# The first loads of a two-block transformer kernel reordered by fourths, with sixteen unread identity products

## The reference

```
mod      = silu(c) @ ada_w + ada_b          # 1024 -> 6144, for c and for c_ctx
h        = rms_norm(x, g) * (1 + scale) + shift     # shift, scale: columns of mod
q, k, v  = split(h @ w_qkv)                 # 1024 x 3072, for x and for ctx
```

## Time and profile before

| | us |
|---|---|
| profiled execution, whole | 1554.06 |
| its span, first to last instruction | 1552.5 |
| TensorE busy | 1519.2 (98%) |
| VectorE busy | 938.1 (60%) |
| ScalarE busy | 705.3 (45%) |
| mean granted clock of TensorE, share of full | 0.997 |

### The profile page before, as it was taken

One profiled execution on the slowest core, in us unless ns is written; L12 is line 12 of the kernel. 1 busy time (PEld: TensorE's weight loads), 2 busy tenths in 40 slices (PEclk: granted clock), 3 DMA queues, 4 the chain that ended last, 5 costly groups with the idle time before them and its releaser, 6 DMA issues.

```text
span 1552.5 us, 21801 instructions
## 1 busy us (share of the span) xinstructions
PE 1519.2 (98%) x9159; PEld 1265.9 (82%) x9159; DVE 938.1 (60%) x1238; ACT 705.3 (45%) x972; POOL 82.0 (5%) x116
## 2 busy tenths in 40 slices
PE   6999999999999999999999999999999999999998
PEld 4777656878888888879778888899988899988887
DVE  5422587463434343356866666678798856679973
ACT  4311475242312222235764545545556546556553
POOL 2010043000000000000010000034000000000000
PEclk8999999999999999999999999999999999999999
DMA  9665432654432332364144555665565554555652
GB/s 360 233 204 166 139 45 73 237 190 136 164 107 82 109 108 69 123 238 142 55 136 136 182 178 177 214 210 184 166 194 186 182 188 149 186 189 179 192 188 81
DMA packets 244161, 251.39 MB, mean 162 GB/s; under 512 B 17134, under 2 KB 237649, under 8 KB 244065
## 3 DMA queue, kind: packets, MB, share of 16 engines
q1 hardware_dynamic: 242528, 247.48, 49.0%
q0 software_dynamic: 928, 1.87, 0.4%
q10 hardware_dynamic: 608, 0.66, 0.1%
HBM read 248.94 MB, written 1.05 MB: 161 GB/s over the span
## 4 chain that ended last, share of the span: by engine, by line
PE 73%; DVE 14%; ACT 5%; issue 2%; POOL 2%; DMA 1%; SPq 1%; POOLq 0%; DVEq 0%; ACTq 0%
PE psum L367 71%; DVE wl L353 6%; ACT wh L346 3%; PE psum L948 2%; DVE scr L2105 1%; DVE scr L2102 1%; DVE scr L2116 1%; DVE scr L2114 1%; DMA pre<-in_ada_w 1%; DVE vsum L2112 1%; ACT scr L2046 1%; DVE sums L1004 1%; POOL ptmp L1868 1%; DMA bias<-in_na_rpb 1%; SPq L293 0%
## 5 line engine op out<-in xcount | busy, mean ns | idle before, releaser
L353 DVE TENSOR_TENSOR wl<-raw,wh 128x2048 fp32r<-128x2048 f32 (+1 forms) x185 | 417.9, 2261 | 261.0 <-ACT wh L346 260.7
L346 ACT ACTIVATE wh<-raw 128x2048 fp32r<-128x2048 f32 (+1 forms) x185 | 347.9, 1883 | 348.7 <-PE psum L367 338.0
L367 PE MATMUL psum<-x,wh 128*128 128x512 f32 (+1 forms) x1440 | 438.8, 365 | 0.8 <-DVE x L549 0.8
L367 PE MATMUL psum<-x,wl 128*128 128x256 f32 x1248 | 350.0, 280 | 0.0
L367 PEld LDWEIGHTS psum<-x,wh 128*128 128x128 f32 x1440 | 258.2, 189 | 46.3 <-issue 1.8
L367 PE MATMUL psum<-xh,wh 128*128 128x512 f32 (+1 forms) x688 | 259.8, 378 | 0.7 <-DVE xl L701 0.7
L367 PE MATMUL psum<-xl,wh 128*128 128x512 f32 (+1 forms) x688 | 255.5, 371 | 0.0
L367 PE MATMUL psum<-xh,wl 128*128 128x512 f32 (+1 forms) x688 | 255.2, 371 | 0.0
L367 PEld LDWEIGHTS psum<-x,wl 128*128 128x128 f32 x1248 | 236.6, 190 | 0.0
L367 PEld LDWEIGHTS psum<-xh,wh 128*128 128x128 f32 x688 | 130.2, 189 | 33.0 <-issue 5.0
L367 PEld LDWEIGHTS psum<-xh,wl 128*128 128x128 f32 x688 | 130.2, 189 | 22.3
(11 more groups left out here) (279 smaller groups left out, 2027.0 us busy)
## 6 DMA issues: line engine op xcount, KB each, us to landing
raw<-in_ffn_w_in SPq DMA_DIRECT2D x44, 1024.0 KB, 5.0
pre<-in_ada_w SPq DMA_DIRECT2D x25, 1024.0 KB, 10.5
raw<-in_ada_w SPq DMA_DIRECT2D x23, 1024.0 KB, 5.7
raw<-in_w_ffn_gate SPq DMA_DIRECT2D x22, 1024.0 KB, 5.1
raw<-in_w_ffn_up SPq DMA_DIRECT2D x22, 1024.0 KB, 5.1
raw<-in_w_ffn_down SPq DMA_DIRECT2D x19, 1024.0 KB, 5.0
raw<-in_ffn_w_out SPq DMA_DIRECT2D x16, 1024.0 KB, 5.0
raw<-in_na_w_qkv SPq DMA_DIRECT2D x12, 1024.0 KB, 5.2
```

The source lines that it names most:

```text
L346: act.e.activation(wh[:, c % NSPL, 0:z], raw[:, p % NRAW, 0:z], ACT.Copy).then_inc(W.hi, 1)
L353: dve.e.tensor_tensor(wl[:, c % NSPL, 0:z], raw[:, p % NRAW, 0:z], wh[:, c % NSPL, 0:z].bitcast(F32), ALU.subtract).then_inc(W.lo, 1)
L367: return pe.e.matmul(o, l, r, start=start, stop=stop, skip_group_check=shared)
```

## The change

The loads are issued in the order x, ctx, ada 0 and 1, a fourth of w0 and w1, ada 2 and 3, a fourth, ada 4 and 5, a fourth, ada 6, ada 7, the last fourth, then w2 and on. A fourth is two k-tiles of both chunks (two loads of 256 KB). The splits follow in fourths (`first_weights`), counted on `J0` for the first three and on `W.hi` and `W.lo` for the last. x is transposed when it has landed, ctx afterwards, in pairs of k-tiles that VectorE copies alone. In TensorE's queue chunks 2 and 3 of `ada_w` go behind the first two k-tiles of c = 0, and so on for each batch. Behind fold 0 stand sixteen products of the identity with itself that nobody reads. `J0` is also used in the second attention layer, where its counts now begin at 6 (`KH`).

```
+            def load_quarter(b):
+                if b >= 2:
+                    sp.wait_ge(J0.hi, 2 * b - 2)
+                for c in range(2):
+                    w, src = (t[:, 2 * b:2 * b + 2, :] for t in (view(raw, c, weights[c]), weights[c][0]))
+                    sp.e.dma_start(w, src).then_inc(s_raw[b % 2], 16)
             for p, (kind, x) in enumerate(dma):
-                if p == 1:
-                    load_staged((2, 3))
-                elif p == 2:
-                    load_staged((4, 5, 6))
+                if p < 2:
+                    continue
+                if p == 2:
+                    for b in range(3):
+                        load_staged((2 * b, 2 * b + 1))
+                        load_quarter(b)
+                    load_staged((6,))
+                elif p == 3:
+                    load_quarter(3)
...
         def setup_pe():
             pe.wait_ge(L.cst, 16)
-            pe.wait_ge(L.row0, 64)
-            pe.e.transpose(bank[6][:, 0:P], vrow[:, 0, :], ident).then_inc(C.turned, 1)
-            pe.wait_ge(L.x, 16)
-            pe.wait_ge(L.ctx, 16)
-            for f in range(KT):
...
+            for a, landed in enumerate((L.x, L.ctx)):
+                pe.wait_ge(landed, 16)
+                for q in range(4):
+                    if a:
+                        pe.wait_ge(X.hT, q + 1)
+                    for m in range(2):
+                        for t in range(2):
...
+                if a == 0:
+                    pe.wait_ge(L.row0, 64)
+                    pe.e.transpose(bank[6][:, 0:P], vrow[:, 0, :], ident).then_inc(C.turned, 1)
             spread_pe(0, 4)
             ada_mm(0)
             ada_mm(1)
             ada_fold(0)
-            ada_mm(2)
-            ada_mm(3)
+            for i in range(16):
+                mm(bank[6][:, 256:384], ident, ident, True, True)
...
         # ScalarE, for each batch b
-            split_hi(0)
+            def first_weights(c, b):
+                q = slice(512 * b, 512 * b + 512)
+                act.wait_ge(s_raw[b % 2], 32 * (b // 2 + 1))
+                act.e.activation(wh[:, c, q], raw[:, c, q], ACT.Copy).then_inc(J0.hi if b < 3 else W.hi, 1)
             for b in range(4):
-                if b == 3:
-                    split_hi(2)
                 modulation(b)
-                if b == 1:
-                    split_hi(1)
+                for c in range(2):
+                    first_weights(c, b)
                 for k in (2 * b, 2 * b + 1):
                     first_high(k)
+            split_hi(2)
...
         # VectorE
+            unmodulated(0)
+            unmodulated(1)
             for b in range(4):
-                if b == 3:
-                    split_lo(2)
                 ada_add(b)
                 first_coefs(b)
...
+                first_normed(2 * b)
+                first_weights(0, b)
+                first_low(2 * b)
+                first_normed(2 * b + 1)
+                first_low(2 * b + 1)
+                first_weights(1, b)
+                if b < 3:
+                    unmodulated(2 * b + 2)
+                    unmodulated(2 * b + 3)
+            split_lo(2)
...
         # qkv0_first_pe
+            for b in range(4):
+                part(0, 2 * b)
+                last = part(0, 2 * b + 1)
+                if b < 3:
+                    ada_mm(2 * b + 2)
+                    ada_mm(2 * b + 3)
+                    part(1, 2 * b)
+                    ada_fold(b + 1)
+                else:
+                    last.then_inc(W.used, 1)
+                    ada_pe(0)
+                    part(1, 2 * b)
+                last = part(1, 2 * b + 1)
+            last.then_inc(W.used, 1)
             ada_pe(1)
```

More of the change, by code:

```diff
@@ L278, in program, with landed @@
         W = semaphores(nc, "w", "hi lo used")
+        def landed(p):
+            return 16 * (p // NRAW + 1) + (48 if p % NRAW < 2 else 0)
         def view(t, slot, src):
@@ L575, in program @@
         C = semaphores(nc, "c", "turned vt act dve")
-        X = semaphores(nc, "x", "tile hT_d hT_a square hn")
+        J0 = semaphores(nc, "split", "hi lo")
+        X = semaphores(nc, "x", "tile hT square hn")
         cf = ins["conv_ffn_2"].rearrange("l k (m p) -> (l k m) p", p=P)
@@ L605, in setup_pe @@
             pe.wait_ge(L.cst, 16)
-            pe.wait_ge(L.row0, 64)
-            pe.e.transpose(bank[6][:, 0:P], vrow[:, 0, :], ident).then_inc(C.turned, 1)
-            pe.wait_ge(L.x, 16)
-            pe.wait_ge(L.ctx, 16)
-            for f in range(KT):
[L611 to L615, removed]
+            for a, landed in enumerate((L.x, L.ctx)):
[5 more added lines that the diff above has]
+                        for t in range(2):
+                            f = 2 * q + m
+                            last = pe.e.transpose(bank[q][:, m * T + t * P:m * T + t * P + P], vtok[:, 2 * a + t, f * P:(f + 1) * P], ident)
+                    last.then_inc(X.tile, 1)
+                if a == 0:
+                    pe.wait_ge(L.row0, 64)
+                    pe.e.transpose(bank[6][:, 0:P], vrow[:, 0, :], ident).then_inc(C.turned, 1)
             spread_pe(0, 4)
@@ L642, in setup_act @@
             act.e.activation(cz[:, :, 30:32].rearrange("p k s -> p s k"), sc.rearrange("p (s k) -> p s k", s=2), ACT.Copy).then_inc(C.act, 1)
-            for f in (5, 7):
-                act.wait_ge(X.tile, f + 1)
-                act.e.activation(hT[:, f, :], bank[f % 4][:, :], ACT.Copy).then_inc(X.hT_a, 1)
             def first_high(k):
@@ L673, in setup_dve @@
             dve.e.tensor_reduce(four[:, :], ident.rearrange("p (j r) -> p r j", j=4), AX.X, ALU.add).then_inc(C.dve, 1)
[L674 to L681, removed]
+            for a in range(2):
+                for q in range(4):
+                    dve.wait_ge(X.tile, 4 * a + q + 1)
+                    dve.e.tensor_copy(hT[:, 2 * q:2 * q + 2, a * T:a * T + T], two(bank[q])).then_inc(X.hT, 1)
+                    if a and q == 1:
+                        recip_dve(0, 4)
+                if a == 0:
+                    dve.wait_ge(C.turned, 1)
+                    dve.e.tensor_copy(vt[:, 0:P], bank[6][:, 0:P]).then_inc(C.vt, 1)
             dve.wait_ge(N.spread, 1)
-            dve.wait_ge(X.tile, KT)
             def unmodulated(k):
-                dve.wait_ge(X.hT_d, min(k + 1, 6))
-                dve.wait_ge(X.hT_a, (k >= 5) + (k >= 7))
+                dve.wait_ge(X.hT, 5 + k // 2)
                 dve.e.tensor_tensor(hn[:, k, :], hT[:, k, :], stat[:, :], ALU.mult).then_inc(X.hn, 1)
@@ L711, in first_normed, with first_weights @@
                                         ALU.add).then_inc(N.scaled, 1)
-            for k in range(4):
-                unmodulated(k)
-            split_lo(0)
+            def first_weights(c, b):
+                q = slice(512 * b, 512 * b + 512)
+                if b < 3:
+                    dve.wait_ge(J0.hi, 2 * b + c + 1)
+                else:
+                    dve.wait_ge(W.hi, c + 1)
+                dve.e.tensor_tensor(wl[:, c, q], raw[:, c, q], wh[:, c, q].bitcast(F32), ALU.subtract).then_inc(J0.lo if b < 3 else W.lo, 1)
+            unmodulated(0)
+            unmodulated(1)
             for b in range(4):
-                if b == 3:
-                    split_lo(2)
                 ada_add(b)
                 first_coefs(b)
[L721 to L731, removed]
+                first_normed(2 * b)
[8 more added lines that the diff above has]
+            split_lo(2)
         B = semaphores(nc, "bias", "in0 in1 masked hi lo")
@@ L765, in qkv0_first_pe, with part @@
             out_ = bank[0:2], bank[2:4]
[L767 to L773, removed]
-                return last
[L776 to L792, removed]
+            def part(c, k):
+                if k >= 6:
+                    h, l = taken(c)
+                else:
+                    pe.wait_ge(J0.lo, k // 2 * 2 + c + 1)
+                    h, l = (view(t, c, weights[c]) for t in (wh, wl))
+                pe.wait_ge(N.xl, 2 * k + 2)
+                for m in range(2):
+                    w = slice(m * P, (m + 1) * P)
+                    last = three(out_[c][m][:, :], h[:, k, w], l[:, k, w], xh0[:, k, :], xl0[:, k, :], k == 0, k == KT - 1)
+                return last
+            for b in range(4):
+                part(0, 2 * b)
+                last = part(0, 2 * b + 1)
+                if b < 3:
+                    ada_mm(2 * b + 2)
+                    ada_mm(2 * b + 3)
+                    part(1, 2 * b)
+                    ada_fold(b + 1)
+                else:
+                    last.then_inc(W.used, 1)
[3 more added lines that the diff above has]
+            last.then_inc(W.used, 1)
             ada_pe(1)
@@ L1047, in program @@
         A0 = semaphores(nc, "att", ATT)
-        J0 = semaphores(nc, "split", "hi lo")
         units0 = [(2 * p + (kind > 0), 2 if kind == 0 else 1, max(kind - 1, 0), 4 * p + (0, 2, 3)[kind]) for p in range(8) for kind in range(3)]
```

7 lines of the change are left out of this document (3 added, 4 removed).

## The result

Thirteen runs of each kernel in turn gave 1558.94 us (1556.78 to 1561.13) for the changed kernel and 1555.62 us (1553.09 to 1556.69) for the one before. The ratio is 1.0026, 95% interval 1.0019 to 1.0033: slower, by 4 us (the medians lie 3.3 us apart). The profiled execution took 1558.94 us with a span of 1557.1, 4.6 us over the span of before.

What follows compares the result with a forecast made beforehand. TensorE, 98% busy, bounds the kernel; only the first 60 us could change. Earlier start and full clock, less batch and load waits, put w2 at 62.2 instead of 58.9: +3.3 on 1555.1 gives 1558.4 us, range 1556.6 to 1560.6 (all cases 1554.0 to 1562.5).

Steps and rivals of the forecast that it cites:

- sixteen products: On TensorE behind fold 0: 1.8 us at the high clock, 16.5 to 18.3, ahead of the first w0 product, costing nothing.
- first w0 product (S0): Start of the first batch's first product on TensorE: at 19.3 us instead of 25.9.
- one batch: Cycle from one batch's first product to the next: 9.38 us, with TensorE waiting 1.3 us for VectorE.
- F3: Moment of VectorE's add behind fold 3, on which w2's late load depends: 44.9 us.
- wait for ada 8: TensorE idle for 4.1 us from 50.3, until ada 8 lands at about 54.4 behind w2.
- wait for ada 9: Second idle stretch of TensorE, 2.5 us from 58.4, until ada 9 lands at 60.9.
- w2's products: First matmul with weight chunk 2, the milestone after which nothing is touched: 62.2 instead of 58.9, +3.3 us.
- the late clock: Rival: low clock before the first w0 product or at ada 9, or a late first load; +6.3, 1561.4 us, chance 0.17.
- Its second form: Clock still low when ada 9 comes, at the first stage's end: up to 1.5 us, within a rival of chance 0.17.
- The chain inside a batch does not bind: Rival: VectorE's and ScalarE's steps overlap better, a cycle takes 8.1 us; +0.7, 1555.8 us, chance 0.12.
- Faster: Rival: late w2, ada 8 and ada 9 loads do not bind the first stage; -3.5, 1551.6 us, chance 0.11.
- The fourth: Rival: before's slower time comes from the first stage's clock, which the change avoids; +3.3 becomes +1, 1557.4 us, chance 0.12.

Runs made afterwards that it cites:

- one: The kernel before with only w2's load issued late and its split at the end of the first stage: 1560.25 us against 1552.80, ratio 1.0048.
- two: The changed kernel with ada 7, 8 and 9 loaded into the buffers of ada 0, 1 and 2, and w2 into raw 2: 1551.45 us, ratio 0.9989 to before.
- ten: The changed kernel with only the fold moved ahead of both k-tiles of c = 1: 1555.78 us against 1554.06 for before, ratio 1.0013.
- nine: The changed kernel with staged loads, eight products and the fold ahead of both k-tiles of c = 1: 1547.79 us, ratio 0.9960 to before.
- three to eight: The changed kernel with none, eight, sixteen, none, eight products, then eight with staged loads; ratios to before 1.0045, 1.0026, 1.0038, 1.0033, 1.0032, 0.9982.
- seven: The changed kernel with eight identity products instead of sixteen, timed again on a second chip: 1557.60 us against 1552.25 for before, ratio 1.0032.

## Why the prediction was right

| step | predicted | changed kernel |
|---|---|---|
| sixteen products | 1.8, hidden | 3.58 (16.68 to 20.26), 0.8 to 0.9 in sight |
| first w0 product (S0) | 19.3 | 20.26 |
| one batch | 9.38 | 9.47, 9.49, 9.48 |
| F3 | 44.9 | 46.08 |
| w2 issued | 46.8 | 48.05 |
| w2 from issue to use | 4.89 | 4.76 |
| its split until ada 9's issue | 4.3 | 4.31 |
| ada 9 from issue to use | 4.89 | 5.25 |
| wait for ada 8 | 4.1 | 4.24 |
| wait for ada 9 | 2.5, less what a low clock takes | 0.80, with 1.7 for the low clock |
| w2's products | 62.2 (+3.3) | 63.56 (+4.6) |

The mechanism held in every step of this profile, and the direction. The first product came early by what was forecast less the products, the batches waited for VectorE, and the time was set by a load, a split and a load behind fold 3. Experiments one, two and ten show the late loads, nine and ten the wait inside a batch, and three to eight what the products cost and keep.

Not all of the nearness is merit. The forecast time, 1558.4 us, is only 0.5 under the measured one, but the milestone moved by 4.6 us where 3.3 were forecast. The medians moved by 3.3 and the ratio says 4.0; with 3 us of noise behind the milestone that agreement is partly luck. The prediction itself gave "slower" a chance of 0.44, no more than "same".

The term that was mis-sized is the sixteen products, 1.8 us instead of 3.58. I priced a product of the identity as a transpose. The trace counts x32 for sixteen: a plain fp32 matmul is two there, each 0.11 us. The rows held this already. A fold is two products in the code and stands as x4, and a pair of `ada_mm` is sixteen in the code and stands as x32. With 3.6 us S0 would have been 20.1, the sum +4.1, and the forecast nearer. It also moved the cover: the products end behind the low part that they fill the time for, so the last 0.8 us of them are on the path. The other misses are the batches (+0.1 each), VectorE's steps behind F3 (1.97 instead of 1.87) and ada 9's load (+0.36), less the small -0.13 of w2's. Some working of the prediction was loose, without weight for the result: 60.9 + 1.0 + 0.2 is 62.1 and not 62.2, and the parts that it gives for its range of +1.5 to +5.5 add up to +2.0 to +6.3.

The clock fell behind the wait of 4.24 us, and in the changed kernel this cost nothing: the low stretch was over at 60.4 and TensorE still waited 0.80 us for ada 9. The first rule of the Trainium skill in the prediction (page "TensorE: Matmul & The Clock Gate", section "HAM oscillation — how this bites in real kernels", on waits for loads) said that it would fall, and the trace agrees. The margin is thin: it was 0.80, 0.52, 0.19 and nothing in four profiles of the changed kernel with sixteen and with eight products. The row at 201 us, taken for the opposite, had a shorter gap. A lone load took 4.76 and 5.25 us here, near the 4.89 of the row. The second rule of the Trainium skill (page "DMA: Bandwidth & Descriptors", section "Anatomy of one DMA") gives 4.4, an estimate by that page, whose figures are for loads that GpSimd issues; these were issued by SyncE.

Of the rivals, the late clock didn't come in this profile: it was at 1.00 from 13 to 56. Its second form, the end of the stage held up by the low clock and not by ada 9, is what seven showed, for about 0.5 us. "The chain inside a batch does not bind" is refuted by the waits of 1.2 us and by experiment nine. "Faster" needed the two waits for loads to stay under 3.3; they were 5.04 and, with the low clock, 6.7. It is what experiment two built. The fourth, that the median of before holds a part that the new kernel loses, found nothing for it: by the ratio the times moved by 4 us, the profiles by 4.6. One sign that the prediction named was missed: the second wait was 0.80 us, at 62, and not 1 to 3 before 61.

What stays open: behind the milestone executions of the same code differ. The changed kernel took 1493.5 us there in one profile and 1491.2 in the other; the eleven experiments lie from 1490.5 to 1493.4, and before had 1493.6. In the first of these two profiles the clock was at its low level for 3.4 us from 1033 on and in the other it was not; that is worth at most 1.7 us, and the rest is not explained. In this noise differences of under 1 us in the first stage are lost. The ratios of 1.0026 and, on another chip, 1.0038 are not told apart either, as their intervals overlap. A small part of the loss lies outside the span: a whole time is 1.8 us more than its span in seven of the thirteen runs of the changed kernel, 2.7 to 3.0 in the other six, and 1.5 to 1.7 in every run of the kernel before beside the experiments. Nothing here shows why. And one repair was not tried, to split the last fourth as soon as it has landed instead of behind VectorE's work for fold 3.

## What to carry to other kernels

When a load's pieces are made finer and its last piece later, ask what waits for the buffer as a whole: here the counter of the whole chunk held the queue for 15 us, and w2, ada 8, w3 and ada 9 were issued 6 to 17 us later than before. Buffers that were free earlier (another slot, ones whose content was used up) repaired it: the ratio went from 1.0026 to 0.9989. And put the instruction that others wait for, here the fold, ahead of the independent work and not in its middle; filler that keeps the clock should end before the work that it bridges to; here sixteen products ended 0.8 us behind it.

## What was not expected of the hardware

Sixteen fp32 products of 128x128 appear as 32 matmuls and take 3.58 us at full clock and 6.5 with most of them at half, against 0.11 us for each transpose. And in these runs filler helped only ahead of the fall. Put in while the clock is still full, eight products (2.0 us, where TensorE otherwise stood for 2.7) kept it there. Put in where it had just fallen, TensorE worked without a break from 19.6 to 26.3 until it was back, and w2 came 1.4 us later than before. How long the low level lasted was not fixed: without products it was 3.4 us in one profile and 6.8 in the other, behind an idle stretch of the same 2.7 us.

The granted clock of 1.00 that the profile shows from the start can't be taken at its word for the first 13 us: in the kernel before, the transposes of the input start 0.21 us apart until 13.1 and 0.11 apart from 13.3 on, as if the first of them ran at the low level.
